# First attention: mixed tiles 0 and 1 made at steps 42 and 44, first output pieces spread over steps 45 to 58

## What is computed

```python
def first_block(x, ...):
    h = rms_norm(x, norm_mix_pre[l])
    proj = h @ w_in[l]
    qa, ka, va, qb, kb, vb = jnp.split(proj, SPLITS, axis=-1)
    qa = apply_rope(rms_norm(qa, q_norm_a), ang_axial)      # 8 heads of 64
    ka = apply_rope(rms_norm(ka, k_norm_a), ang_axial)      # 2 key heads
    out_a = global_attention(qa, ka, va)                    # every key
    qb = apply_rope(qb, ang_1d); kb = apply_rope(kb, ang_1d)
    out_b = window_attention(qb, kb, vb, sink_b)            # keys within 128, with a sink
    mixed = concatenate([rms_norm(out_a, group_norm_a),
                         rms_norm(out_b, group_norm_b)]) @ w_out
    x = x + rms_norm(mixed, norm_mix_post)
    ...                                                     # gated feed-forward
```

## Time and profile before

| | us |
|---|---|
| median of 3 runs | 1087.11 |
| the three runs | 1087.57, 1085.83, 1087.11 |
| the profiled execution's own time | 1084.58 |
| its span, first to last instruction | 1082.7 |
| PE busy in it | 1060.9 (98%) |
| DVE, ACT, POOL busy | 885.1, 667.1, 186.3 |

### The profile page before, as it was taken

How to read it: one execution, slowest core, us unless ns; L and a number is a source line. 1 busy time by engine, 2 the same in 40 slices (tenths; PEclk the granted TensorE clock), 3 DMA queues, 4 the chain that set the end, 5 groups by cost and what they waited for, 6 DMA issues and landing times.

```text
span 1082.7 us, 17989 instructions
## 1 busy us (share of the span) xinstructions
PE 1060.9 (98%) x6544; PEld 936.5 (86%) x6544; DVE 885.1 (82%) x1440; ACT 667.1 (62%) x1171; POOL 186.3 (17%) x239
## 2 busy tenths in 40 slices
PE   8999988999999999999999999999999999999997
PEld 6688866998999999988888787788899999998886
DVE  6888895798998888798775688756689888879876
ACT  7787785476555555656684468745445555556664
POOL 1486745011101111100000103300001110110000
PEclk9999999999999999999999999999999999999999
DMA  7422320657676766886546620154356576676553
GB/s 288 115 79 73 99 64 26 241 134 185 201 167 198 203 174 189 213 237 199 181 161 200 171 76 12 40 143 169 97 137 184 205 174 188 186 194 213 196 184 128
DMA packets 51319, 171.16 MB, mean 158 GB/s; under 512 B 6432, under 2 KB 7072, under 8 KB 51104
## 3 DMA queue, kind: packets, MB, share of 16 engines
q1 hardware_dynamic: 37296, 122.56, 34.5%
q0 software_dynamic: 13312, 46.14, 19.2%
q10 hardware_dynamic: 624, 1.31, 0.4%
HBM read 162.64 MB, written 48.23 MB: 195 GB/s over the span
## 4 chain that ended last, share of the span: by engine, by line
PE 86%; DVE 6%; ACT 3%; issue 2%; POOL 1%; DMA 1%; ACTq 0%; SPq 0%; DVEq 0%; POOLq 0%
PE bank L2135 11%; PE bank L2134 11%; PE bank L2133 11%; PE bank L2694 6%; PE bank L2696 6%; PE bank L2695 6%; PE bank L613 6%; PE bank L614 6%; PE bank L615 6%; PE bank L1180 2%; PE bank L1170 2%; PE bank L1125 1%; PE bank L1126 1%; PE bank L1127 1%; DVE wl L535 1%
## 5 line engine op out<-in xcount | busy, mean ns | idle before, releaser
L535 DVE TENSOR_TENSOR wl<-raw,wh 128x1024 fp32r<-128x1024 f32 (+1 forms) x144 | 170.0, 1186 | 60.2 <-ACT wh L522 58.8
L522 ACT ACTIVATE wh<-raw 128x1024 fp32r<-128x1024 f32 (+1 forms) x145 | 145.9, 1010 | 110.7 <-PE bank L2696 50.3
L2133 PE MATMUL bank<-h,wh 128*128 128x256 f32 x576 | 163.0, 283 | 0.0
L2134 PE MATMUL bank<-h,wh 128*128 128x256 f32 x576 | 163.0, 283 | 0.0
L2135 PE MATMUL bank<-h,wl 128*128 128x256 f32 x576 | 163.0, 283 | 0.0
L2134 PE MATMUL bank<-hl,wh 128*128 128x256 f32 x432 | 122.3, 283 | 0.0
L2135 PE MATMUL bank<-hh,wl 128*128 128x256 f32 x432 | 122.3, 283 | 0.0
L2133 PE MATMUL bank<-hh,wh 128*128 128x256 f32 x432 | 122.2, 283 | 0.0
L2694 PE MATMUL bank<-wh,high_tokens 128*128 128x512 f32 x308 | 121.1, 393 | 0.0
L2696 PE MATMUL bank<-wh,low_tokens 128*128 128x512 f32 x308 | 120.0, 390 | 0.0
L2695 PE MATMUL bank<-wl,high_tokens 128*128 128x512 f32 x308 | 119.9, 389 | 0.0
(11 more groups left out here) (345 smaller groups left out, 2653.7 us busy)
## 6 DMA issues: line engine op xcount, KB each, us to landing
raw<-weights SPq DMA_DIRECT2D x163, 512.0 KB, 4.2
down_weight_sums<-weights POOLq DMA_DIRECT2D x60, 512.0 KB, 5.8
raw<-down_weight_sums SPq DMA_DIRECT2D x40, 512.0 KB, 4.2
down_weight_sums<-down_weight_sums POOLq DMA_DIRECT2D x20, 512.0 KB, 4.5
xres<-x_t SPq DMA_DIRECT2D x8, 512.0 KB, 7.2
down_weight_sums<-weights POOLq DMA_DIRECT2D x12, 256.0 KB, 4.9
sw<-ta SPq DMA_DIRECT2D x36, 64.0 KB, 2.0
raw<-down_weight_sums SPq DMA_DIRECT2D x8, 256.0 KB, 2.6
```

The costliest lines, as they stand in the source:

```text
L522: act.activation(wh[:, j, b, n], raw[:, j, b, n], ACT.Copy).then_inc(high_split, 1)
L535: v.tensor_tensor(wl[:, j, b, :], raw[:, j, b, :], wh[:, j, b, :].bitcast(F32), ALU.subtract)\
L2133: pe.matmul(o, wh_half[:, h, k, :], high[:, k, :], start=first and k == 0, stop=False, skip_group_check=True)
L2134: pe.matmul(o, wh_half[:, h, k, :], low[:, k, :], start=False, stop=False, skip_group_check=True)
```

## The change

The entries of two tables and the place of one buffer are changed. The high parts of mixed tiles 0, 1 and 2 are made at steps 42, 44 and 50 (before: 49, 50 and 51), their low parts one step later. The first eight output pieces are issued at steps 45, 46, 48, 50, 52, 54, 56 and 58 (before: one at every step from 52 to 59). The low parts of tiles 0 and 1 move to the place of `hsq`; there they wait for tile 7 of the projection to be done, where before they waited for tile 11. Tiles 3 to 7, and the pieces from step 65 on, keep their steps. No work is added or removed.

```diff
-MIX.update({0: 49, 1: 50, 2: 51})
+MIX.update({0: 42, 1: 44, 2: 50})
 
-OUT_PIECES = {52: [(0, 0)], 53: [(1, 0)], 54: [(0, 1)], 55: [(1, 1)], 56: [(0, 2)], 57: [(1, 2)], 58: [(0, 3)], 59: [(1, 3)],
+OUT_PIECES = {45: [(0, 0)], 46: [(1, 0)], 48: [(0, 1)], 50: [(1, 1)], 52: [(0, 2)], 54: [(1, 2)], 56: [(0, 3)], 58: [(1, 3)],
               65: [(0, 4)], 66: [(1, 4)], 67: [(0, 5)], 68: [(1, 5)], 71: [(0, 6)], 72: [(1, 6)]}
...
-        mix_l0 = place("mix_l0", [P, 4, S], F32R, at=arena + 32 * KB)
+        mix_l01 = place("mix_l01", [P, 2, S], F32R, at=arena + 84 * KB)
+        mix_l23 = place("mix_l23", [P, 2, S], F32R, at=arena + 32 * KB)
...
         def mix_low(k):
-            return mix_l0[:, k, :] if k < 4 else mix_1[:, k - 4, 1, :]
+            return mix_l01[:, k, :] if k < 2 else mix_l23[:, k - 2, :] if k < 4 else mix_1[:, k - 4, 1, :]
...
         def vec_mix_low(v, i):
             v.wait_ge(mixsplit1.high, MIX_ORDER.index(i) + 1)
-            if i < 4:
+            if i < 2:
+                v.wait_ge(f1.done, DONE_ORDER.index(NORMED[-1]) + 1)
+            elif i < 4:
                 v.wait_ge(f1.done, len(DONE_ORDER))
```

## The result

| | kernel before | changed kernel |
|---|---|---|
| median of 20 runs each, alternating | 1085.22 us (1084.6 to 1087.57) | 1088.48 us (1086.09 to 1091.09) |
| profiled execution | 1084.58 us | 1088.85 us |
| its span | 1082.7 us | 1087.0 us |
| mean granted clock of TensorE in it | 0.999 | 0.996 |

The ratio is 1.0025, with a 95% interval of 1.0018 to 1.0032: the change makes the kernel slower by about 2.7 us (0.25%); the two medians lie 3.26 us apart. The forecast was no change, with a small gain. By the two profiled executions the kernel is 4.27 us longer. Of that, 0.66 us lie ahead of step 42, and 0.57 of these ahead of the first scores (38.53 and 39.10 us), before anything that the change touches. Another 3.65 us lie between the scores of step 42 and the sum over the query heads at step 71: the row of the sum is

A forecast was written before the change was run, and what follows sets the result against it. PE was taken as the bound, busy 98% of the span. PE's +0.15 and DVE's middle of -0.15 gave nothing; small unplaced waits gave -0.2, so 1087.11 - 0.2 = 1086.9 us, range 1084.8 to 1088.6.

The forecast's parts named there:

- Pieces out of the full stretch: Four output pieces move from steps 52 on to PE's idle time at steps 45 to 50; alone worth 2.8 us.
- High and low parts: Moved to steps 42 to 45, they make DVE 1.8 us late by the reductions of blocks 46 to 50.
- POOL's chain: Reciprocals at step 45 come 1.15 us later, POOL's products take 0.4 more; rope of tile 11 ends at 146.4, not 144.81.
- The new end of the first stretch: Low part 2 ends at 151.6; step 52's piece starts at 151.7, 3.15 us later, PE idling some 2.5 there.
- A wait for a low part at steps 45 to 50: Sign of a wrong forecast: PE waiting at steps 45 to 50 for tile 1's low part or the weights.
- The second stretch: Steps 53 to 62: late piece +3.15, four fewer pieces -2.8, small waits -0.2, so PE +0.15 us at step 60.
- DVE would use 1 us of its own waits: In steps 53 to 62, DVE recovers about its 0.5 to 1.0 us lateness from 1.76 us of idle time.
- The rivals: Three alternatives: DVE's waits absorb everything (1085.2, chance 0.25), DVE pays for the shared port (1088.4, 0.15), nothing arrives (1087.1, 0.10).
- The faster rival: Step 52's piece doesn't hold PE, as POOL's chain comes only 0.5 us late: -1.9, 1085.2 us; chance 0.25.
- The chance of 0.75 for no change: Probability given to a measured time within 0.2% of before, between 1084.9 and 1089.3 us.
- the slower rival: At step 45 POOL's products hold DVE at the shared port, each low part taking 1.47 us: 1088.4 us; chance 0.15.

The follow-up runs named there:

- e1_warm: Changed kernel with 12 products of a zero tile put before the output piece of step 52, where PE stood idle; 1086.06 us, ratio to before 1.0007.
- a2_after: The changed kernel once more, unedited, run beside two others on the same chip; 1087.84 us, ratio to before 1.0018.
- e7_later: Kernel before with its first eight pieces spread to steps 52, 53, 54, 56, 58, 60, 62, 63, no tile moved; 1085.0 us, ratio 0.9992.
- e4_mix_only: Changed kernel with the eight pieces back at steps 52 to 59, its early high and low parts kept; 1086.4 us, ratio to before 1.0010.
- the best two versions: Changed kernel with high parts at 46, 49, 51 and pieces from 49 to 63; then also tail pieces at 68, 70; ratios 0.9982 and 0.9974.
- e3_late_low: Kernel before with high parts 0, 1, 2 one step later (50, 51, 52), all pieces where they were; 1087.85 us, ratio 1.0021.
- e6_mix1_46: Changed kernel with high part 1 at step 46 and low part 1 at step 47; 1087.09 us, ratio to before 1.0018.
- e9_low0_47: Changed kernel with high parts at 46, 49, 51 and pieces at 49, 50, 52, 54, 56, 58, 61, 63; 1083.84 us, ratio to before 0.9982.

## Why the prediction was wrong, step by step

**Pieces out of the full stretch: right.** They found room at steps 45 to 50 with one wait of 0.32 us, and PE did 1.5 us more work in the first stretch.

**High and low parts: right in kind, small in size.** DVE waits 0.91 for `pth`, where 0.29 + 0.5 = 0.8 was forecast. Block 50's reduction starts at 147.83 - 0.66 = 147.17, which is 2.21 us later than in the earlier trace rows, not 1.8. Part of the missing 0.4 is the low part of tile 4 at 140.96, which took 0.97 us beside POOL's products and not 0.72.

**POOL's chain: the products right, the rope add mis-sized.** The reciprocals came 1.29 us late (forecast 1.15) and the products took 2.90 us (forecast 2.46 + 0.4). The rope add, which I left at 2.41, took 2.86. This is +0.45 on a chain with no slack: it ended 2.2 us late, not 1.55.

**The new end of the first stretch: right in mechanism, short in size.** The piece started at 153.10 - 0.66 = 152.44, 3.9 us later than the first piece in the earlier trace rows, where 3.15 was forecast; 0.65 of the 0.75 us come from the rope add and the rest of POOL's chain. The wait was 2.88 us for a forecast of 2.5. By the forecast's own times it would be 151.7 - 149 = 2.7; and the 3.8 - 2.8 us of idle time that it names as the wait's source come to 1.0, so that most of the wait is the late piece. A wait for a low part at steps 45 to 50 was named as a sign of being wrong; the one that came, 0.32 us at step 45, was small.

**The second stretch: the step that failed.** The sum there was +3.15 - 2.8 - 0.2 = +0.15 at step 60. With the measured 3.9 it would have been +0.9, and e1_warm, where the clock holds, measures +1.16 at the sum of step 71. Steps 53 to 62 were to take some 2.5 us less than 15.3; from the scores of step 53 to those of step 63 they take 12.71 us in e1_warm and 14.58 in the changed kernel. So the terms of the sum were right to about a quarter of a microsecond once the wait had its size. Missing was a term: I counted the wait as time in which PE does nothing and let PE go on behind it at the pace of the earlier trace rows. The granted clock was read in those rows (1.00 everywhere) and taken for constant. It fell to 0.50 in this wait, and the difference between the changed kernel and e1_warm, 2.49 us, is its cost in the profiled execution (1.30 in that of a2_after). That DVE would use 1 us of its own waits behind the piece failed for the same reason: at half clock it got more to wait for (1.88 us before block 53's reduction).

**The rivals.** None of the three came. DVE was not held for 1.47 us per low part; where the port was contended at step 45, POOL was the one that paid most. The faster rival's condition, POOL's chain only 0.5 us late, was not met by far. The slower side lacked the mechanism that decided: its rival should have been "the wait of 2.5 us before step 52 lets the clock fall", which the forecast's own wait made possible. The chance of 0.75 for no change leant on the missing term.

**Luck in the number.** The measured median, 1088.48, is within the range given and beside the slower rival's 1088.4. Neither says anything for the forecast: that rival's mechanism didn't come, and all these times were counted from 1087.11, the median of three runs of before, where 20 runs have 1085.22. Counted from there, the forecast is 1085.0 and the range 1082.9 to 1086.7, and the measured time lies outside.

**Of the clock in the medians.** Each run's record gives its mean granted clock. In the 20 runs of the changed kernel it is 0.994 to 0.996 in eleven (median 1089.81 us) and 0.997 to 0.999 in nine (1087.39). The kernel before has differences of this sort too: over 86 runs of it, those at 0.998 or more have a median of 1084.89, the others lie over 1 us higher. Where its clock fell in those isn't known, since none was profiled; the falls at the first scores in e1_warm and e7_later show one place where it can. All runs of e1_warm are at 0.998 or more, and their median, 1086.06, is 1.2 us over that of before, which agrees with its profile's +1.16. The changed kernel has one run at 0.999, and it took 1086.09 us: the same 1.2 us over before. That fits an execution without a fall, but it wasn't profiled.

## What to carry to other kernels

The price of a wait on TensorE is its length and the pace of the products behind it: when a change gathers several short waits into one long one, ask what the granted clock does there, and put a product that is ready (here the scores of the next step) ahead of the one that waits. When early work is moved, the queue that it is moved past sets the price, not the one that it is meant to relieve: by e4_mix_only the low parts cost 1.2 us behind steps 42 and 44, where DVE had no slack and POOL hung on it, and the best two versions make the first high part only at step 46. Most of the gain came from spreading the pieces over the waits that were already there, up to the tail: 0.92 us in e7_later, which moves nothing else, and another 0.95 by the two pieces of the tail. And read where the granted clock fell before two profiles are compared: one execution of a kernel can have a fall that the next has not.

## What the hardware showed that I had not expected

**TensorE's clock can fall within a wait of under 3 us, and the length of the wait alone doesn't decide it.** At the piece of step 52 it fell from 2.4 to 1.2 GHz in each of the three profiles with a wait of 2.88 or 2.97 us (two of the changed kernel, one of e3_late_low), and it stayed at 1.2 for 3.4 us once and for 6.8 twice, with PE busy for most of that time. It didn't fall in the one profile with 2.32 us there, nor at 1.60, 1.26 or 1.17. But it also fell at the first scores in two of the 13 profiles, e1_warm (waits of 1.16 and 0.54 us just before) and e7_later (1.35 and 0.28), and stayed at 1.2 for over 3 us; the kernel before has waits of 1.09 and 0.61 at the same place and keeps its clock. So a short wait is no safe wait, and what tells these executions apart no run shows.

The Trainium skill (Advanced Engine Details and Errata, Clock Domains) says that the array's clock is gated to 1.2 GHz when it is idle. The three falls within the long waits agree, with windows in which PE did nothing; the two at the first scores came with PE at work again. e1_warm, whose twelve products add zero to a bank and change nothing else, shows that work without use held the clock at step 52. What decides how long the half clock lasts was not tried, nor was whether e6_mix1_46 has falls at step 52 in executions that weren't profiled. Its median of 1087.09, which is 1.5 us over before, is more than the 0.91 us of its profiled stretch, which would fit some falls but doesn't show them.

**Of two engines that meet at the port, either can be the one that pays, and half a microsecond decides.** Four readings of the same two DVE and POOL instructions (us):

| | POOL rope add | DVE weight split | start of the split behind that of the rope add |
|---|---|---|---|
| kernel before | 2.41 | 1.21 | 0.07 |
| changed kernel | 2.86 | 1.21 | 0.51 |
| e6_mix1_46 | 1.56 | 1.57 | 1.06 |
| e9_low0_47 | 1.55 | 1.57 | 1.07 |

POOL's four products at step 45 took 2.46 us beside one low part and 2.90 beside two; the next four took 2.05 us before. It needn't be a low part: in the changed kernel those next four, at 148.01, took 2.48 us with none beside them, but with the rope part L1393 at 149.22, which reads two SBUF tiles too and itself took 0.92 us instead of 0.76. In e6_mix1_46 a low part of DVE took 1.04 us instead of 0.74, at 143.64, across the end of POOL's L1524 and the start of the rope add.

The Trainium skill (SBUF — State Buffer, Who interferes with whom) calls the shared port pair an exclusive lock and has the issue order decide which engine is blocked. The rows agree that the two engines hold each other up and that the order matters. They don't agree in who pays: by its start the rope add is first in all four, and in the first two it is the one that gets longer, by 1.12 and 1.57 us over the 1.29 that the same shape took at 133.92 in the earlier trace rows. (POOL's times in a profile are rough.) So a row of before gives the price of a meeting but not the payer: both sides of it belong in the range.
